# Sample value products in four 32-column strips, dilated scores on alternating row halves

## Time and profile before

| | |
|---|---|
| timed runs | 724.51 us median (723.68 to 726.27) |
| profiled execution | 723.28 us |
| its span, first to last instruction | 721.3 us |
| mean granted TensorE clock | 0.951 of full speed |
| TensorE busy (products) | 652.8 us, 91% |
| TensorE weight loads (beside products) | 592.7 us, 82% |
| VectorE busy | 357.4 us, 50% |
| ScalarE busy | 248.0 us, 34% |
| GpSimd busy | 175.6 us, 24% |
| DMA | 98.42 MB, mean 136 GB/s |

### The profile page before, as it was taken

One profiled execution on the slowest core, in us unless ns is written; L12 is line 12 of the kernel. 1 busy time (PEld: TensorE's weight loads), 2 busy tenths in 40 slices (PEclk: granted clock), 3 DMA queues, 4 the chain that ended last, 5 costly groups with the idle time before them and its releaser, 6 DMA issues.

```text
span 721.3 us, 12479 instructions
## 1 busy us (share of the span) xinstructions
PE 652.8 (91%) x4740; PEld 592.7 (82%) x4740; DVE 357.4 (50%) x759; ACT 248.0 (34%) x539; POOL 175.6 (24%) x187
## 2 busy tenths in 40 slices
PE   2989999999999999999898788999999899847992
PEld 2688999899898999999898787665599899746992
DVE  1864455555545443444576763221147532492762
ACT  5552343433434324333122133121113332555410
POOL 3513010010100400003488770101002222375000
PEclk9799999999999999999999999999979999878997
DMA  8069462552521771341599966464423320223112
GB/s 239 8 172 348 149 204 51 185 190 74 183 56 41 236 243 50 88 118 30 160 303 319 312 170 192 117 181 145 145 75 110 88 66 24 74 73 88 45 45 60
DMA packets 105545, 98.42 MB, mean 136 GB/s; under 512 B 6355, under 2 KB 93703, under 8 KB 105200
## 3 DMA queue, kind: packets, MB, share of 16 engines
q1 hardware_dynamic: 101872, 71.64, 34.6%
q0 software_dynamic: 3568, 25.99, 10.0%
q10 hardware_dynamic: 48, 0.01, 0.0%
HBM read 90.31 MB, written 26.14 MB: 161 GB/s over the span
## 4 chain that ended last, share of the span: by engine, by line
PE 70%; DVE 10%; DMA 5%; ACT 3%; issue 3%; SPq 3%; POOL 3%; POOLq 0%; DVEq 0%; ACTq 0%
PE pj L790 47%; PE tr L782 5%; PE pv L740 4%; PE pv L926 3%; DMA kv_b<-in_cache_b_kv_dram 3%; PE sc L893 3%; PE sc L901 2%; PE pv L744 2%; DVE w_lo L1315 1%; DVE yT L1687 1%; PE sc L790 1%; DMA x_in<-in_x_prompt_dram 1%; POOL prod L623 1%; DVE xT L1688 1%; PE sc L898 1%
## 5 line engine op out<-in xcount | busy, mean ns | idle before, releaser
L790 PE MATMUL pj<-h_hi,w_hi 128*128 128x260 f32 x1088 | 323.3, 297 | 30.9 <-ACT gsig L1134 11.6
L790 PE MATMUL pj<-h_lo,w_hi 128*128 128x260 f32 x1088 | 312.9, 288 | 0.0
L790 PE MATMUL pj<-h_hi,w_lo 128*128 128x260 f32 x1088 | 312.7, 287 | 0.0
L790 PEld LDWEIGHTS pj<-h_hi,w_hi 128*128 128x128 f32 x1088 | 211.0, 194 | 46.5 <-issue 31.0
L790 PEld LDWEIGHTS pj<-h_lo,w_hi 128*128 128x128 f32 x1088 | 211.2, 194 | 0.0
L790 PEld LDWEIGHTS pj<-h_hi,w_lo 128*128 128x128 f32 x1088 | 210.7, 194 | 0.0
L1315 DVE TENSOR_TENSOR w_lo<-w_raw,w_hi 128x1024 fp32r<-128x1024 f32 (+1 forms) x76 | 92.9, 1226 | 59.0 <-ACT w_hi L1061 58.4
L1061 ACT ACTIVATE w_hi<-w_raw 128x1024 fp32r<-128x1024 f32 (+2 forms) x84 | 81.5, 973 | 95.9 <-PE pj L790 39.9
L1322 DVE COPY probT<-tr 128x256 f32<-128x256 f32 (+3 forms) x56 | 27.4, 489 | 51.1 <-PE tr L782 51.1
L623 POOL TENSOR_TENSOR prod<-kv_a,qbc 128x512 f32<-128x512 f32 x24 | 33.7, 1433 | 18.5 <-DMA kv_b<-in_cache_b_kv_dram 13.5
L926 PE MATMUL pv<-v_tok,probT 128*128 128x64 f32 x216 | 29.4, 263 | 0.0
(11 more groups left out here) (328 smaller groups left out, 966.0 us busy)
## 6 DMA issues: line engine op xcount, KB each, us to landing
w_raw<-in_w_in_dram SPq DMA_DIRECT2D x52, 512.0 KB, 4.7
kv_a<-in_cache_a_kv_dram SPq DMA_DIRECT2D x64, 256.0 KB, 3.6
out_dram<-in_cache_b_kv_dram POOLq DMA_DIRECT2D x16, 1022.0 KB, 9.7
qbc<-q_dram SPq DMA_DIRECT2D x8, 640.0 KB, 5.4
kv_b<-in_cache_b_kv_dram SPq DMA_DIRECT2D x32, 128.0 KB, 3.1
w_raw<-in_w_out_dram SPq DMA_DIRECT2D x8, 512.0 KB, 3.8
w_raw<-in_w_ple_gate_dram SPq DMA_DIRECT2D x8, 512.0 KB, 4.1
x_in<-in_x_prompt_dram SPq DMA_DIRECT2D x4, 512.0 KB, 6.0
```

The costliest lines, as they stand in the source:

```text
L790: ins = nc.tensor.matmul(out, w[:, k0, :], x[:, c_x, lo:hi], start=first and i == 0, stop=last and i == 2)
```

## The change

Two parts of TensorE's work get other places in the array.

**Values.** The 8 samples become two sets (SETS) of four strips (STRIPS). Sample s = 4k + j writes its 8 (branch B: 4) rows of output to partitions 32j onward of bank pv[k] (branch B: of sc[1], 256 columns for each set). The probabilities are no longer padded. A step sample_pages(f) does page p of four samples; sample_slots(f) does one group's window of four samples. The accumulation of a set begins with the new token's product, whose weights d_a and d_b are padded to 32 columns per sample, so that it writes all 128 partitions. SP loads by the same steps: value_pages(f) four pages, one of each sample, value_slots(f) four windows, each two steps ahead at most. The page steps 0 to 5 follow the tiles t = 13 to 18, the window steps 0 to 4 the tiles t = 14 to 18; steps 6, 5 and 7 stand ahead of the first branch tile. The mask and the channels are done per set, on 128 partitions.

**Scores.** For branch B both heads stay where the projection leaves them, partitions 0 to 63 and 64 to 127 of q_two and k_two, which overlay q_aug and k_aug; k_two serves the transposes as well. scores_two issues the scores of both heads of a pair at even steps, alternating between the heads, one PSUM bank for each, behind the projection part of the step and not ahead of it; it waits until the maxima of the previous two units are done.

The diff's core (constants, semaphore names and some buffers are left out; head_a and head_b become masks by i % 32, strip is 1 where i // 32 is the strip). No line of it touches the bias generator.

```diff
 
+            def value_pages(f):
+
+                k, p = divmod(f, PAGES)
+                if f >= 2:
+                    sp.wait_ge(S["s_vpa"], f - 1)
+                for j in range(STRIPS):
+                    at = PAGES * (STRIPS * k + j) + p
+                    page = sp.value_load(pt[0:1, at:at + 1], min_val=0, max_val=POOL_PAGES - 1)
+                    src = A["cache_a_kv"][0, bass.ds(page, 1), :, 1, :, :].rearrange("o t h d -> (o t) (h d)")
+                    sp.dma_start(kv_a[f % 2][:, j, :], src).then_inc(S[f"s_kp{f % 2}"], 16)
+
+            def value_slots(f):
+
+                k, g = divmod(f, BG)
+                if f >= 2:
+                    sp.wait_ge(S["s_vsl"], f - 1)
+                n, step = SLOTS[g], DIL[g]
+                for j in range(STRIPS):
+                    src = caches[g][0, STRIPS * k + j, 0:n * step:step, 1, :, :].rearrange("t h d -> t (h d)")
+                    sp.dma_start(kv_v[f % 2][0:n, j, :], src).then_inc(S[f"s_kv{f % 2}"], 16)
 
             sp.wait_ge(s_pt, 16)
...
+            value_pages(0)
             load(n + 3)
-            sample_rows(1, 1)
+            value_pages(1)
+            value_slots(0)
             load(n + 4)
+            value_slots(1)
             load(n + 5)
             n += 6
-            for s in range(2, DEC):
-                sp.wait_ge(S["s_samp"], s - 1)
-                sample_rows(s, 1)
+            for f in range(2, SETS * PAGES):
+                value_pages(f)
+                if f < SETS * BG:
+                    value_slots(f)
                 load(n)
                 n += 1
-            sp.wait_ge(S["s_os"], 1)
+            sp.wait_ge(S["s_vsl"], SETS * BG)
+            sp.wait_ge(S["s_vpa"], SETS * PAGES)
             sp.wait_ge(S["s_sst"], 16 * 8)
             sp.dma_start(p_in[:, :, :], A["p_prompt"][0, 0].rearrange("(b p) d -> p b d", p=P)).then_inc(S["s_pin"], 16)
             sp.dma_start(ps_in[:, :], A["p_sample"][0].rearrange("s o d -> (s o) d")).then_inc(S["s_pin"], 16)
...
+        new_v = st[:, :, :].rearrange("s (r j) c -> s j r c", j=3)[:, 2]
+
+        def sample_pages(pe, f):
+
+            k, p = divmod(f, PAGES)
+            if f == 0:
+                pe.wait_ge(s_used, USE_ROW + 4)
+                pe.wait_ge(S["s_dv"], 2)
+            if p == 0:
+                nc.tensor.matmul(pv[k][:, :], d_a[:, STRIPS * k:STRIPS * (k + 1), :].rearrange("s t x -> s (t x)"), new_v[:, 0:ROUNDS_A, :],
+                                 start=True, stop=False, skip_group_check=True)
+            pe.wait_ge(S[f"s_kp{f % 2}"], 64 * (DEC // 2 + f // 2 + 1))
+            for j in range(STRIPS):
+                s = STRIPS * k + j
+                last = nc.tensor.matmul(pv[k][32 * j:32 * j + AH, :], pTa[:, p, s * AH:(s + 1) * AH], kv_a[f % 2][:, j, :],
+                                        start=False, stop=p == PAGES - 1, skip_group_check=True)
+            last.then_inc(S["s_vpa"], 1)
+
+        def sample_slots(pe, f):
+
+            k, g = divmod(f, BG)
+            n, r0, cols = SLOTS[g], ROUNDS_A + 2 * g, slice(k * BO, (k + 1) * BO)
+            nc.tensor.matmul(sc[1][:, cols], d_b[:, g, STRIPS * k:STRIPS * (k + 1), :].rearrange("s t x -> s (t x)"), new_v[:, r0:r0 + 2, :],
+                             start=g == 0, stop=False, skip_group_check=True)
+            pe.wait_ge(S[f"s_kv{f % 2}"], 64 * (f // 2 + 1))
+            for j in range(STRIPS):
+                s = STRIPS * k + j
+                last = nc.tensor.matmul(sc[1][32 * j:32 * j + BH, cols], pTb[0:n, g, s * BH:(s + 1) * BH], kv_v[f % 2][0:n, j, :],
+                                        start=False, stop=g == BG - 1, skip_group_check=True)
+            last.then_inc(S["s_vsl"], 1)
 
         def sample_channels(pe):
 
-            pe.wait_ge(S["s_osm"], 2)
-            for cc in range(AW // P):
-                nc.tensor.matmul(pv[0][:, cc * DEC:(cc + 1) * DEC], os_a[:, cc * P:(cc + 1) * P], cst("row_a", 64), start=True, stop=True)
-            for cc in range(BO // P):
-                last = nc.tensor.matmul(pv[0][:, 32 + cc * DEC:32 + (cc + 1) * DEC], os_b[:, cc * P:(cc + 1) * P], cst("row_b", 32), start=True, stop=True)
+            pe.wait_ge(S["s_osm"], 2 * SETS)
+            for k in range(SETS):
+                s0, s1 = STRIPS * k, STRIPS * (k + 1)
+                for cc in range(AW // P):
+                    nc.tensor.matmul(pv[0][:, cc * DEC + s0:cc * DEC + s1], os_a[:, k, cc * P:(cc + 1) * P], cst("strip"), start=True, stop=True)
+                for cc in range(BO // P):
+                    last = nc.tensor.matmul(pv[0][:, 32 + cc * DEC + s0:32 + cc * DEC + s1], os_b[:, k, cc * P:(cc + 1) * P], cst("strip"), start=True, stop=True)
             last.then_inc(S["s_ot"], 1)
 
...
-                elif qb is not None:
-                    k0 = max(qb - 1, 0) * P
-                    n = (qb + 1) * P - k0
-                    last = nc.tensor.matmul(b[:, 0:n], q_aug[s][0:HD, hd, qb * P:(qb + 1) * P], k_aug[s][0:HD, hd, k0:k0 + n], start=True, stop=True)
-                else:
-                    for c in range(CLS):
-                        last = nc.tensor.matmul(b[:, c * P:(c + 1) * P], q_aug[s][0:HD, hd, c:SEQ:CLS], k_aug[s][0:HD, hd, c:SEQ:CLS], start=True, stop=True)
-                last.then_inc(s_sc, 1)
...
+            def scores_two(r, i):
+                qb = units(r)[i][1]
+                u = unit0[r] + i
+                s = (r - 1) % 2
+                q, k = q_two[s], k_two[s]
+                rows = [slice(hd * HD, (hd + 1) * HD) for hd in range(2)]
+                if i == 0:
+                    pe.wait_ge(s_free[0], 3 * r)
+                    pe.wait_ge(s_free[1], 3 * r)
+                pe.wait_ge(s_ex if u == unit_a else s_mx, u)
+                if qb is not None:
+                    k0, k1 = max(qb - 1, 0) * P, (qb + 1) * P
+                    for hd in range(2):
+                        nc.tensor.matmul(sc[(u + hd) % 2][:, 0:k1 - k0], q[rows[hd], qb * P:k1], k[rows[hd], k0:k1], start=True, stop=True).then_inc(s_sc, 1)
+                    return
+                for c in range(CLS):
+                    for hd in range(2):
+                        ins = nc.tensor.matmul(sc[(u + hd) % 2][:, c * P:(c + 1) * P], q[rows[hd], c:SEQ:CLS], k[rows[hd], c:SEQ:CLS], start=True, stop=True)
+                        if c == CLS - 1:
+                            ins.then_inc(s_sc, 1)
 
             def blocks(r, qb):
                 return qb + 1 if is_a(r) else CLS if qb is None else min(qb, 1) + 1
...
                             turn([(P, b * P, vT[:, b * P:(b + 1) * P]) for b in range(NB)])
                         else:
                             turn([(P, c * P, vT[:, c:SEQ:CLS]) for c in range(CLS)])
-                    if i < nu:
+                    if i < nu and is_a(r):
                         scores(r, i)
                     if i:
                         project(3 * r + i // 4, i % 4)
+                    if i < nu and not is_a(r) and i % 2 == 0:
+                        scores_two(r, i)
                     if r == 0 and i == 9:
                         pe.wait_ge(S["s_logf"], 1)
...
@@ -979,11 +1030,10 @@
                     sample_rows_t(pe, turn)
                 if t == 12:
                     sample_probs_t(pe, turn)
-                if 13 <= t < 17:
-                    sample_values(pe, t - 13)
-                if t >= 17:
-                    sample_values(pe, 2 * t - 30)
-                    sample_values(pe, 2 * t - 29)
+                if t >= 13:
+                    sample_pages(pe, t - 13)
+                if t >= 14:
+                    sample_slots(pe, t - 14)
 
             for m in range(DC):
                 n = TILE_BR + m
@@ -991,7 +1041,9 @@
                 for half, cols in enumerate(HALVES):
                     pe.wait_ge(s_free[half], n)
                     if m == 0 and half == 0:
-                        sample_end(pe)
+                        sample_pages(pe, 6)
+                        sample_slots(pe, 5)
+                        sample_pages(pe, 7)
                     if m == 0 and half == 1:
                         sample_channels(pe)
                         pe.wait_ge(S["s_ogsl"], 1)
...
+                    if j < 2 and r >= ROUNDS_A:
+                        last = nc.scalar.activation((k_two if j else q_two)[s][:, 0:HALF], ps[:, 0:HALF], ACT.Copy, scale=1.0 if j else SCALE)
...
+            dve.wait_ge(S["s_vsl"], SETS * BG)
+            dve.wait_ge(S["s_vpa"], SETS * PAGES)
             heads = lambda b, n: b.rearrange("r (h d) -> r h d", h=n)
-            V.tensor_tensor(heads(os_a[:, :], AH), heads(pv[0][0:DEC * AH, :], AH), cst("head_a", 64).unsqueeze(2).to_broadcast([64, AH, HD]), ALU.mult).then_inc(S["s_osm"], 1)
-            V.tensor_tensor(heads(os_b[:, :], BH), heads(pv[1][0:DEC * BH, 0:BO], BH), cst("head_b", 32).unsqueeze(2).to_broadcast([32, BH, HD]), ALU.mult).then_inc(S["s_osm"], 1)
+            for k in range(SETS):
```

(29 more changed lines are left out.)

62 lines of the change are left out of this document (24 added, 38 removed).

## The result

The changed kernel takes 697.43 us (median of 4 runs, 695.39 to 698.74) beside 724.1 for the kernel before (4 runs, 721.95 to 726.27): a ratio of 0.963, 95% interval 0.959 to 0.967. The profiled execution took 695.39 us, its span is 693.4, and the span before was 721.3. So 27.9 us went, where 12.6 were forecast.

The account below looks back on a forecast made before the run. TensorE, busy throughout the touched stages, was taken as the bound. Terms -11.3 (values), +2.1 (wait), +2.0 (channels), -2.6 (first rounds) and -2.8 (last rounds) gave -12.6: 710.7 us profiled, 711.9 beside the timed median; range 699 to 730.

Parts of the forecast that it names:

- Page step 2.30, window step 1.31: Value stage: partly overlapping products make a page step 2.30 us and a window step 1.31, from 3.58 without overlap for pages.
- five slots: Value stage: with starts in program order, four two-instruction products take 5 slots of 0.427 us in a page step.
- New token 5.6: Value stage: the new token's products opening every accumulation, with their changes of tile shape, cost 5.6 us.
- The wait of 2.1 at step 7: End of value stage: TensorE waits 2.1 us for page step 7's load, whose buffer step 5 must free.
- full overlap: Rival, value stage: starts pass each other, page step 1.02, window step 0.67; sum -24.1, 700.4 us; chance 0.15.
- Clock in the value stage: Rival: clock falls after new token's products in six value stages, 9.4 us in all; 721.3 us; chance 0.06.
- Channels +2.0: End of value stage: 24 channel instructions for 12 cost 2.8 us more at low clock, nothing at full; 2.0 taken.
- First two dilated rounds -2.6: Scores there: a pair of heads in one go takes 0.83 us with overlap against 1.24; 2.6 us won.
- Last four rounds -2.8: Scores there: 1.2 us from earlier transposes plus 1.6, half of two clock falls; 2.8 won, between 1.2 and 4.3.
- The rival on the weight loads: Last four rounds: strips overlap, weight loads of row halves don't; +6.0 in place of -2.8, 720.7 us; chance 0.20.
- The rest at nothing: Evacuations in rounds 5 to 10, POOL's memsets and copies, and the bias generator change the time by nothing.
- the middle two: Rivals with row halves' weight loads apart (chance 0.20) and clock falling in the value stage (0.06); three quarters counted as faster.

Follow-up runs that it names:

- two_aabb: Changed kernel, but a page step takes two samples with two pages each, order A, A', B, B', instead of four samples with one page; 697.98 us (0.965).
- pages_ahead: Changed kernel with SP's queue reordered: pages of step 6 ahead of window loads, pages of step 7 ahead of three weight loads; 695.94 us (0.961).
- same_rows: Changed kernel with its new order of scores, but both heads stay on rows 0 to 63, with the evacuations of before; 705.92 us (0.975).
- values_only: The value part of the change alone, with the score code of the kernel before; 707.59 us (0.977).
- scores_only: The score part of the change alone, with the value code of the kernel before; 711.51 us (0.984).
- heads_in_turn: Changed kernel, but rounds 7 to 10 issue all classes of head 1, then all of head 2, instead of alternating heads; 698.9 us (0.965).

## Why the prediction was wrong, point by point

**Page step 2.30, window step 1.31: wrong, and this is the step that failed.** They rested on "if a start may not pass an earlier one", and on the five slots that follow from it. Measured are 0.97 and 0.55, which is two slots, and `two_aabb` shows that a start does pass up to three that wait for another strip. The bounds had been set right (1.02 and 3.58), and the value between was taken from the one rule that no row of before bore on. The Trainium skill ("TensorE: Matmul & The Clock Gate", Part 3) says that starts and ends keep program order; here the starts don't, and the measurement decides. The Trainium skill ("TensorEngine Tiling (Array Packing)", Theoretical Speedup), with its up to 4x, stood nearer: 3.58 / 0.97 is 3.7. With 0.97 and 0.55 in place, the forecast's own sum for eight page steps and six window steps falls from 26.3 to 11.1. With the new token (5.8), the waits (5.1) and the lower clock in steps 6 and 7 and the window step between them (some 2.8) it comes to 24.8, which is what the stage's value work and waits take now where they took 43.2.

**New token 5.6: right.** 2 x 1.05 and 6 x 0.62 are 5.8.

**The wait of 2.1 at step 7: mis-sized, and one of two.** It is 5.1 us, at steps 6 and 7. "Earlier steps have a projection tile of some 6 us twice between release and use" is not so for step 6, which has one tile there. And the pages were taken to go out 0.75 after their buffer is free, as before; they go out 4.2, 6.1, 5.4 and 5.5 us later at steps 3 to 6, behind window loads that wait for a later step of TensorE, and one step hands its lateness on to the next, for the queue needs as long as a step of TensorE. Two tiles cover that, one doesn't. `pages_ahead` shows that it is the order: with the pages first, step 6 doesn't wait. The rival "full overlap" had 4.7 for it, near the sum, but at one place.

**Clock in the value stage.** The rival expected six falls behind the new token's products; there is none up to 488. One came, behind the wait of step 6. Steps 6 and 7 paid 0.93 each for it, and window step 5 between them about as much.

**Channels +2.0: wrong.** 24 instructions in 2.59 for 12 in 2.76: the clock, low beside them in the earlier trace rows, was at 1.00 over 498.40 to 501.70. The price "nothing more at full clock" was the right one of the two. The half tile costs 0.5 more, 3.65 for 3.13.

**First two dilated rounds -2.6: half of it.** A pair takes 0.63 where two units took 1.26, and not 0.83: two slots again and not three. Six are 3.7 by their starts, and the two pairs of block 0, at 0.42 for 0.64, bring 0.4 more. A further 1.2 had no term: value products that are no longer followed by scores start 0.12 closer to what comes next (0.14 and 0.37 for 0.26 and 0.49). Against it stand some 0.7, of which 0.4 is the first projection part of each round: the step behind it starts 0.2 later each time, in a wait for the first pair's exponential. That the pairs' softmax is covered by one part held for the rest.

**Last four rounds -2.8: right in mechanism, short in size.** 16 scores take 2.21; the forecast had "If they do, 9 slots make 2.3 us". They do, for the loads of both halves start within 10 ns of each other. That 2.3 came so near is luck in one respect: the starts come in pairs here too, eight slots and not nine, 0.233 apart after a first of 0.42. The gain without clock is 0.28 in rounds 7 and 9, as 0.3 foreseen, and both falls went where I had counted half of them. By `same_rows` it isn't the order that took them away. The rival on the weight loads leaned on a misreading: the rows themselves had loads of 0.325 that start 0.25 apart, so in the trace one load already starts before the last has ended.

**The rest at nothing: right.** No wait for VectorE's masks, POOL's copies or the evacuations shows in the chain. Of the -0.8 elsewhere, the projection tile ahead of t = 13 takes 5.98 where it took 7.49. The granted clock was 0.50 in its first half before (435.40 to 438.80) and is 1.00 throughout it now; `values_only` and `scores_only` both have 5.98 too, so either part is enough; why the fall isn't there stays open.

**The rival that came near.** "Full overlap" (700.4) had the right mechanism in the value stage, and a chance of 0.15. Its distance of 3 us is smaller than its errors: it had -20.7 for the value stage with its wait and +2.0 for the channels, where -18.4 and +0.3 were measured, and took 3.7 less from the rounds than they gave. In the chances, forecast, full overlap and three quarters of the middle two make 0.72, not "some 0.70"; nothing hangs on it.

## What to carry to other kernels

When operations may overlap and no row shows how, bound them and let the extreme cases carry real weight: a rule about order is a guess until a trace with two operations in two strips has been read. When a stage gets shorter, follow the queue that feeds it in its own order: a load whose buffer is free still stands behind loads that wait for theirs, and that shows first where the least work lies between release and use. Before a load is moved back, follow who converts it and what is queued behind that conversion on each engine.

## What was not expected of the hardware

- A 512-column fp32 product is two instructions 0.43 apart, and those of other strips start beside it, 7 ns (four strips) or 14 ns (two) after one another. In the page steps, in `two_aabb` and in `heads_in_turn` an instruction passed three waiting ones; in the last, where more stood there, it did not pass a fourth.
- Eight weight loads of 8 columns in four strips over the same 128 rows took 0.12 us together, where one takes 0.085 to 0.089.
- Two strided weight loads of 0.327 us each, on the two row halves, run at the same time: 16 scores in 2.21 us.
- A page costs SP about 1.1 us to issue, of which 0.42 is reading its number from the table, so four keep it for 3.67 from the first issue to the end of the last; a page is on its way for 2.6 to 4.0, 3.1 in the median. Here the issue of a step takes as long as the transfer of a page.
